# Feed-forward products of two layers as seven quarter products instead of eight (Strassen's scheme), in rounds of 4, 6, 6 and 6 chunks

## The reference, cut to what matters

```python
D_FF = 2816
def swiglu(h, w_gu, w_down):
    gu = h @ w_gu                       # (512 x 1024) @ (1024 x 5632)
    g, u = gu[..., :D_FF], gu[..., D_FF:]
    return (jax.nn.silu(g) * u) @ w_down # (512 x 2816) @ (2816 x 1024)

for i in range(2):
    h = h + (dilated_mixer if i == 0 else forgetting_mixer)(rmsnorm(h, ...), ...)
    h = h + swiglu(rmsnorm(h, ffn_norm[i]), ffn_w_gu[i], ffn_w_down[i])
return rmsnorm(h, final_norm)
```

## Time and profile before

| | |
|---|---|
| median of 3 runs | 2414.19 us (2409.96 to 2414.33) |
| the profiled execution | span 2408.6 us |
| PE busy | 2300.8 us, 96% |
| DVE, ACT, POOL busy | 983.4, 967.8 and 946.0 us, 39 to 41% |
| feed-forward of layer 0 | 1396.2 to 1746.8 us of the span |
| feed-forward of layer 1 | 2052.0 to 2402.6 us of the span |
| DMA | 316 MB, mean 131 GB/s |

### The profile page before, as it was taken

The page is one execution under the profiler, slowest core; times in us unless marked ns, Lnnn a source line. Parts: engine busy times, 40 slices in busy tenths (PEclk is TensorE's granted clock), DMA queues, the critical chain, the costliest instruction groups (busy, mean ns, idle before and its releaser), DMA issues.

```text
span 2408.6 us, 31104 instructions
## 1 busy us (share of the span) xinstructions
PE 2300.8 (96%) x11626; PEld 1871.0 (78%) x11626; DVE 983.4 (41%) x1651; ACT 967.8 (40%) x1611; POOL 946.0 (39%) x757
## 2 busy tenths in 40 slices
PE   7999999888888999999998899999999999999998
PEld 6886786444447998999987688888878887888887
DVE  4377446889884233362235621111311124111113
ACT  4344524656664344344343442222344444322223
POOL 4442141535562333323332145454432222544542
PEclk9999999999999999999998999999999999999999
DMA  5521146999975222322321132333332211333332
GB/s 181 171 87 36 53 163 228 358 390 402 383 310 185 77 88 94 103 69 75 101 89 56 38 103 92 101 96 97 102 106 74 71 53 53 91 102 95 97 100 84
DMA packets 211612, 316.24 MB, mean 131 GB/s; under 512 B 19936, under 2 KB 141536, under 8 KB 201648
## 3 DMA queue, kind: packets, MB, share of 16 engines
q1 hardware_dynamic: 203760, 301.97, 36.5%
q0 software_dynamic: 7744, 12.76, 1.6%
HBM read 300.89 MB, written 22.71 MB: 134 GB/s over the span
## 4 chain that ended last, share of the span: by engine, by line
PE 80%; DVE 6%; DMA 5%; ACT 3%; issue 3%; POOL 1%; SPq 1%; DVEq 0%; ACTq 0%; POOLq 0%
PE bank L868 22%; PE bank L870 21%; PE bank L869 21%; DMA w_ring<-in_w_gate 5%; PE bank L1494 2%; PE bank L1120 2%; PE bank L907 2%; DVE up_low L2555 2%; PE bank L1099 1%; PE bank L1471 1%; POOL w_low L3072 1%; PE bank L1110 1%; PE bank L1481 1%; PE bank L1308 1%; PE bank L1292 1%
## 5 line engine op out<-in xcount | busy, mean ns | idle before, releaser
L3072 POOL TENSOR_TENSOR w_low<-raw,w_high 128x512 fp32r<-128x512 f32 x568 | 743.1, 1339 | 1173.6 <-ACT w_high L1731 1141.8
L868 PE MATMUL bank<-h_high,w_high 128*128 128x512 f32 x1088 | 429.6, 395 | 2.3 <-DVE h_low L2299 2.3
L870 PE MATMUL bank<-h_high,w_low 128*128 128x512 f32 x1088 | 424.4, 390 | 0.0
L869 PE MATMUL bank<-h_low,w_high 128*128 128x512 f32 x1088 | 424.0, 390 | 0.0
L1731 ACT ACTIVATE w_high<-raw 128x2048 fp32r<-128x2048 f32 x145 | 277.0, 1910 | 256.9 <-PE bank L870 237.4
L868 PE MATMUL bank<-w_high,h_high 128*128 128x512 f32 (+2 forms) x832 | 327.9, 394 | 7.7 <-DVE h_low L2299 3.2
L870 PE MATMUL bank<-w_high,h_low 128*128 128x512 f32 (+2 forms) x832 | 312.1, 375 | 0.0
L869 PE MATMUL bank<-w_low,h_high 128*128 128x512 f32 (+2 forms) x832 | 311.8, 375 | 0.0
L868 PEld LDWEIGHTS bank<-h_high,w_high 128*128 128x128 f32 x1088 | 204.6, 188 | 47.2 <-DVE h_low L2299 6.1
L870 PEld LDWEIGHTS bank<-h_high,w_low 128*128 128x128 f32 x1088 | 204.4, 188 | 43.2
L869 PEld LDWEIGHTS bank<-h_low,w_high 128*128 128x128 f32 x1088 | 204.6, 188 | 40.0
(11 more groups left out here) (380 smaller groups left out, 3376.2 us busy)
## 6 DMA issues: line engine op xcount, KB each, us to landing
raw<-in_ffn_w_gu SPq DMA_DIRECT2D x88, 512.0 KB, 4.5
raw<-in_a_w_in SPq DMA_DIRECT2D x72, 512.0 KB, 4.7
w_ring<-in_w_gate SPq DMA_DIRECT2D x35, 1024.0 KB
w_ring<-in_w_up SPq DMA_DIRECT2D x35, 1024.0 KB
w_ring<-in_w_down SPq DMA_DIRECT2D x35, 1024.0 KB, 9.1
raw<-in_ffn_w_down SPq DMA_DIRECT2D x40, 512.0 KB, 4.6
raw<-in_w_in SPq DMA_DIRECT2D x34, 512.0 KB, 4.6
raw<-in_b_w_in SPq DMA_DIRECT2D x24, 512.0 KB, 4.6
```

The source lines that it names most:

```text
L868: pe.matmul(out, sta[0], mov[0], start=start, stop=False)
L869: pe.matmul(out, sta[0], mov[1], start=False, stop=False)
L870: return pe.matmul(out, sta[1], mov[0], start=False, stop=stop)
L3072: last = pool.tensor_tensor(out=w_low[:, slot, cols], in0=raw[:, slot, cols], in1=w_high[:, slot, cols].bitcast(F32), op=ALU.subtract)
```

## The change

A product of two matrices that are cut into 2 x 2 quarters takes eight products of quarters; Strassen's scheme (in Winograd's form) takes seven, of sums of quarters, and combines them with more additions. The new kernel does so for the feed-forward products of 20 of the 22 chunks going up and of all 11 pairs of chunks going down. The first two chunks of a layer (`FF_PLAIN`) go up as before.

**Up.** A chunk's block is a 2 x 2 of (rows 0 to 511, rows 512 to 1023) by (gate, up); h is a 2 x 2 of row halves by token halves. Each of the seven products has 4 k-steps of 128x128 weights on 256 tokens, in three passes. **Down.** A pair of chunks by the two column halves of the down matrix; each product has, for two tiles of 128 tokens, one k-step of 512 columns per pair.

- VectorE makes sums of weight quarters (four 128x512 per chunk; three and a late one per pair), and per layer four sums of quarters of h with their low parts. It combines the seven results in PSUM with 256-wide adds per chunk, and with 22 adds of 128x512 per down round. It makes the sums of the activations per pair of chunks (`act_full`, seven 128x256 and their low part).
- The split parts of weights no longer lie in whole blocks but in a ring of seven quarters of 128x512 (`ring_high`, `ring_low`). ScalarE makes each high part; the low part comes from VectorE for quarters 1 and 2 of an up chunk and 1, 3, 5 of a down pair (`VECTOR_LOW`), otherwise from GpSimd. Each engine's order is one unrolled pass over `FF_QUADS`: at quarter q ScalarE splits q+7, VectorE combines q, makes low parts of q+5 and sums for q+7.
- Rounds are 4, 6, 6, 6 chunks. The down weights of the odd chunks' right and left halves are loaded again for the late quarters, so a layer has 42 blocks for 34.
- Some semaphores are shared by what had its own, the forget gate's weights `fw_raw` and the last gain `gw2` lie elsewhere, tokens are normed in the order 2, 3, 0, 1 after a feed-forward.

```diff
-FF_ROUNDS = [8, 8, 6]
+FF_ROUNDS = [4, 6, 6, 6]
+FF_PLAIN = 2
...
+FF_QUADS = []
+for _r, _chunks in enumerate(FF_ROUNDS):
+    for _c in range(0 if _r else FF_PLAIN, _chunks):
+        FF_QUADS += [("up", _r, _c, _j) for _j in range(7)]
+    for _i in range(_chunks // 2):
+        FF_QUADS += [("down", _r, _i, _j) for _j in range(4)]
+    for _j in range(4, 7):
+        FF_QUADS += [("down", _r, _i, _j) for _i in range(_chunks // 2)]
+VECTOR_LOW = {"up": (1, 2), "down": (1, 3, 5)}
+    ring_high = at("ring_high", 45, [P, 7, 512], F32R)
+    ring_low = at("ring_low", 61, [P, 7, 512], F32R)
...
+            def up_quad(r, c, j):
...
+                quad_ready(q)
...
+                else:
+                    pe.wait_ge(up_read, up0 - 7 + [1, 1, 2, 4, 5, 6, 7][j])
...
+                for k in range(4):
...
+                    last = pass3(out, (wh[:, k, :], wl[:, k, :]), mov, k == 0, k == 3)
+                last.then_inc(quad_used, 1)
...
+            def down_part(r, i, j, tile):
...
+                sta = [x[:, i, ACT_PLACE[j], tile * P:(tile + 1) * P] for x in (act_high, act_low)]
+                return pass3(bank[DOWN_BANKS[j] + tile][:, :], sta, (quad_place(ring_high, q), quad_place(ring_low, q)),
+                             i == 0, i == FF_ROUNDS[r] // 2 - 1)
...
+            def quad_high_part(q):
+                if q >= 7:
+                    act.wait_ge(quad_used, q0 + q - 6)
...
+                act.activation(quad_place(ring_high, q), quad_full(l, q), ACT.Copy).then_inc(quad_high, 1)
...
+            def up_sums(r, c):
...
+                add(s1, a21, a22).then_inc(quad_sum, 1)
+                quad_summed(("up", r, c, 3))
+                sub(s2, s1, a11).then_inc(quad_sum, 1)
+                sub(a21, a11, a21).then_inc(quad_sum, 1)
...
+            def quad_low_part(q):
...
+                dve.wait_ge(quad_high, q0 + q + 1)
+                sub(quad_place(ring_low, q), quad_full(l, q), quad_place(ring_high, q).bitcast(F32))\
+                    .then_inc(vector_low, 1)
...
+            def gated_sums(f):
...
+                step(add(act_full[:, 5, :], act_full[:, 0, :], act_full[:, 4, :]))
+                step(sub(act_full[:, 6, :], act_full[:, 5, :], act_full[:, 1, :]))
+                sub(act_full[:, 7, :], act_full[:, 3, :], act_full[:, 6, :]).then_inc(ff_sums, 1)
...
+            def up_result(r, c, j):
...
+                if j == 1:
+                    add(up_u2[:, :], out, up_first[:, :]).then_inc(up_read, 1)
...
+                elif j == 3:
+                    dve.wait_ge(up_read, up0 + 2)
+                    add(up_c22[:, :], out, up_u3[:, :]).then_inc(up_read, 1)
+                    dve.wait_ge(ff_silu, 2 * f)
+                    add(up_c12[:, :], out, up_u2[:, :]).then_inc(up_read, 1)
...
+            for q in range(FF_N):
+                what, r, i, j = FF_QUADS[q]
+                if what == "up" and j > 0:
+                    up_result(r, i, j)
+                if what == "down":
+                    down_result(r, i, j)
...
+                if q + 7 < FF_N and FF_QUADS[q + 7][3] == 0:
+                    (up_sums if FF_QUADS[q + 7][0] == "up" else down_sums)(*FF_QUADS[q + 7][1:3])
+                if q + 8 < FF_N and FF_QUADS[q + 8][0] == "down" and FF_QUADS[q + 8][3] == 5:
+                    down_last_sum(*FF_QUADS[q + 8][1:3])
+                if q + 5 < FF_N and FF_QUADS[q + 5][3] in VECTOR_LOW[FF_QUADS[q + 5][0]]:
+                    quad_low_part(q + 5)
+                if q + 3 < FF_N and FF_QUADS[q + 3][0] == "up" and FF_QUADS[q + 3][3] == 0:
+                    up_last_sum(*FF_QUADS[q + 3][1:3])
...
+        def quad_lows(l):
+            for q, (what, _, _, j) in enumerate(FF_QUADS):
+                if j not in VECTOR_LOW[what]:
+                    pool.wait_ge(quad_high, FF_N * l + q + 1)
+                    pool.tensor_tensor(out=quad_place(ring_low, q), in0=quad_full(l, q),
+                                       in1=quad_place(ring_high, q).bitcast(F32), op=ALU.subtract).then_inc(pool_low, 1)
```

More of the change, by code:

```diff
@@ L794, in ffn_loads @@
         def ffn_loads(l):
-            w_gu, w_dn = by_k(a["ffn_w_gu_2"][l]), a["ffn_w_down_2"][l]
+            w_gu, w_dn = by_k(a["ffn_w_gu_2"][l]), by_k(a["ffn_w_down_2"][l])
             for r, chunks in enumerate(FF_ROUNDS):
                 n0 = B_FFN[l] + FF_BLOCK[r]
[L799 to L805, removed]
+                pairs = chunks // 2
+                f0 = FF_CHUNK[r]
+                for c in range(chunks):
+                    n = n0 + c
+                    dst = shaped(raw, n % 2, 8)
+                    col = P * (f0 + c)
+                    load(n, n % 2, [(dst[:, :, 0:P], w_gu[:, :, col:col + P]),
+                                    (dst[:, :, P:2 * P], w_gu[:, :, FF + col:FF + col + P])])
                 if l == 0 and r == 0:
@@ L908, in turn, with first_turns @@
             last.then_inc(turned, 1)
-        def first_turns(rows, ready, clock=True):
+        def first_turns(rows, ready, clock=True, order=tuple(range(NT))):
             for m in range(chunk[0], chunk[0] + 2):
@@ L1552, in swiglu @@
         def swiglu(l):
-            for r, chunks in enumerate(FF_ROUNDS):
[L1554 to L1611, removed]
@@ new lines, in swiglu, with first_block @@
+            n0 = B_FFN[l]
+            def first_block(k):
+                if l == 0 and k < 6:
+                    pe.wait_ge(q_low, 3 + k // 2 + 1)
+                elif k == 0 or l == 0:
+                    block_ready(n0)
+                wh, wl = weights(n0 % 2, 8)
+                for m in range(2):
+                    cc = slice(m * P, (m + 1) * P)
+                    last = pass3(PLAIN_BANKS[0][m][:, :], (wh[:, k, cc], wl[:, k, cc]),
+                                 (h_high[:, k, :], h_low[:, k, :]), k == 0, k == KD - 1)
+                if k == KD - 1:
+                    last.then_inc(ff_out, 1)
@@ new lines, in swiglu @@
+            dve.wait_ge(turn_free, chunk[0])
+            for k in range(2):
+                part = slice(4 * k, 4 * k + 4)
+                step(add(h_full[:, part, :], h_high[:, part, :].bitcast(F32), h_low[:, part, :].bitcast(F32)))
+            b11, b12 = h_full[:, 0:4, 0:256], h_full[:, 0:4, 256:512]
+            b21, b22 = h_full[:, 4:8, 0:256], h_full[:, 4:8, 256:512]
+            t1, t2, t3, t4 = [t_full[:, i, :, :] for i in range(4)]
+            sub(t1, b12, b11).then_inc(ff_sums, 1)
```

594 lines of the change are left out of this document (461 added, 133 removed).

## The result

The changed kernel takes 2577.28 us (median of four, 2574.97 to 2578.71) against 2414.26 (2409.96 to 2414.45) for the one before, run beside it: ratio 1.0686, 95% interval 1.067 to 1.0702. The forecast was 2497, its own range 2440 to 2555; the range for 8 in 10, 2370 to 2580, just holds the result. Direction, place and mechanism were as predicted; the loss, 163 us, is twice the 83 forecast.

What follows compares the result with a forecast made beforehand. TensorE's matmul stream bounds the old kernel; in the new one VectorE, stopped by GpSimd's SBUF reads, takes 392 us per layer, 41.4 more than 350.6. Two layers add 83 to 2414.2: 2497 us, range 2440 to 2555, 8 in 10 2370 to 2580.

Steps and rivals of the forecast that it cites:

- The step that failed: Feed-forward stages: VectorE, with GpSimd's stops, paces each layer at 392 us, 41.4 more than 350.6.
- VectorE alone: Feed-forward of a layer: VectorE's own sums, low parts and adds take 291 us, beside TensorE's 320.
- stopped by GpSimd: Feed-forward of a layer: 144 GpSimd instructions each stop VectorE's two-operand SBUF work for 0.70 us.
- VectorE idle: Feed-forward of a layer: VectorE's waits got no term in the 392 us, though full resources were said not to meet without waits.
- w: Feed-forward stages: time one GpSimd instruction stops VectorE, taken as 0.70 us, forecast range 0.50 to 0.90.
- Four prices: VectorE's chunk: stop 0.97 with a two-operand instruction behind, about 0.6 with a lone PSUM add, 0 with three, about 0.65 during PSUM adds.
- The down rounds of three: Down rounds of three pairs: VectorE needs 26.2 us alone, beside 28.6 of TensorE, before GpSimd's stops.
- Rival 2: Feed-forward stages: VectorE and GpSimd alternate strictly, w = 0.97, 431 us per layer, 2575 us; chance 0.11.
- Rival 1: Feed-forward stages: TensorE stays the bound, w at most 0.2, 2358 us; chance 0.18 with its tail up to no change.
- TensorE's 320 us: Feed-forward of a layer: TensorE's matmuls by quarters take 320 us, 30.5 less than before.
- The clock: Granted clock falls with TensorE's idle time; called small, 0.94 to 1.00 at 81 to 88% busy; within a 0.06 rival over 2585 us.
- The forecast's upper case: Each GpSimd instruction stops VectorE for all its 1.26 us: 472 us per layer, 2658 us; a third of a 0.06 chance.

Runs made afterwards that it cites:

- the sums spread: Changed kernel with act_low issued last in its step, plus an up chunk's three weight sums issued in three steps instead of one: 2562.55 us, ratio 1.0637.
- the port free: Changed kernel with GpSimd's quarter low parts replaced by memsets that read no SBUF: 2393.82 us, ratio 0.9928 against the kernel before.
- TensorE alone: Changed kernel with GpSimd's low parts as memsets, and most of VectorE's weight sums cut to 8 of 512 columns: 2387.86 us, ratio 0.9903.
- the better one: Only down products by quarters, all 22 up chunks plain; GpSimd makes a round's first seven low parts, VectorE the others: 2438.35 us, ratio 1.0114.

## Why the prediction was wrong in size

**The step that failed** is the sum "VectorE sets the pace: 291 + 144 x 0.70 = 392 us per layer". It measured 436.5 in layer 0, and the runs split it into its terms:

| term, layer 0 | forecast | measured | from |
|---|---|---|---|
| VectorE alone | 291 | 299.8 | busy time with GpSimd writing only |
| stopped by GpSimd | 101 | 113.0 | busy time of the changed kernel less that |
| VectorE idle | 0 | 23.7 | window less busy time |

That is +9, +12 and +24. (The forecast's prices for dependent instructions hold a gap of 0.04 each, which the last row counts as idle, so the border between the rows isn't sharp.) Both stages together are 436.5 + 432.3 - 2 x 392 = 84.8 us over, and the time 80.

- **Idle time was set at nothing**, and it is the largest piece. A resource that sets the pace was taken to be never idle. The prediction itself wrote that resources full "in any order can't meet without waits", and gave that no price. 9.4 us are waits for ScalarE's high part ahead of act_low, 6.1 for TensorE's results in the down rounds. It is no accident of one order: 20.7 us with act_low last, 24.1 (426.35 - 402.22) with the sums spread, 22.6 with all low parts on VectorE, 29.4 with all on GpSimd. But the waits differ: with all on VectorE 7.6 us of them are late loads, which the changed kernel has none of.
- **w was 0.76 to 0.78, not 0.70** (per 148 or per the 144 counted). In the up chunks alone it is 0.87: ten GpSimd instructions per pair lengthen ten sums and low parts (7.36 us in the chunk shown and 8.14 in the next, in place of 10 x 0.684) by 8.7 us. All 512-wide ones with two SBUF operands last 1.14 in the mean (forecast near 1.0). Four prices under it failed. An instruction directly behind another two-operand one was to lose 0.97, one behind a lone PSUM add 0.6: in the chunk shown they lose 1.09 and 0.76 (1.77 and 1.44 in place of 0.68). Longer runs of PSUM adds were to cover the stop whole; spreading the sums showed that it falls on the next two-operand instruction instead. And all adds of down results were priced as PSUM adds, while 32 of a layer's are X<-down_u with two SBUF operands: 32 x (918 - 683) = 7.5 us.
- **VectorE alone** was 3% short. That the 0.09 by which independent instructions overlap isn't reached in every place is a guess; no run shows it. From the measured 299.8, 144 more instructions at the forecast's 0.60 came out within 2% (386 for 380.0).
- **What held:** VectorE busy over 85% (95%); TensorE waiting for VectorE's low parts, not for GpSimd, ScalarE or loads; 256-wide PSUM adds at 0.42; 256-column matmuls 0.12 apart; GpSimd's 128x512 over 1.5 (1.63). The down rounds of three, 35.1 for 34.6, are in part luck, since the slowed X<-down_u weren't in their price.
- **Rival 2** named 2575 us, 2 from the result, for another reason: strict alternation at w = 0.97. The slowest sums do last 1.77 in the trace, but the mean is 0.76 and the rest is idle time.
- **Rival 1** (2358) had more against it than the port: with the port free 2393.8, and with TensorE alone 2387.9. That TensorE's 320 us would be met but for late starts was too low by 17 a layer.
- **The clock** was called small. It was granted at 0.91 and 0.90 in the two stages, where TensorE mostly didn't set the pace. In one place it did: at the end of round 0 TensorE had waited 7.11 us for act_low, its next matmuls ran 0.43 apart at a granted clock of 0.50 (1453.5 to 1459.0; that is the 1.2 GHz level) in place of 0.23, and VectorE waited 4.86 us for their result, the longest of its waits:

```profile
1454.13 0.79 PE L978 MATMUL bank<-ring_high,act_high 128*128 128x512 f32 x1 [7.11 <-DVE act_low L2486]
```
```profile
1459.54 1.29 DVE L2483 TENSOR_TENSOR X<-down_u,X 128x512 f32<-128x512 f32 x2 [4.86 <-PE bank L980]
```

What stays open: of the remaining 8.2 us of VectorE's idle time in layer 0, 1.5 are a wait for ScalarE's root at the end, the rest some 110 gaps of 0.11 us or less, whose cause isn't shown. Open, too, is whether the down half alone could win with the squares ahead of the split and GpSimd's plain blocks held back. By an estimate from the waits shown that would give back about 4 us each a layer, not enough for the 27 that the better one lacks. It wasn't tried.

## What to carry to other kernels

Trading matmuls for elementwise work moves the bound to VectorE; price that work with GpSimd's SBUF reads beside it, and count for each instruction how many operands lie in SBUF, the copies that were made to free PSUM too. A low part given to GpSimd cost VectorE 0.7 to 0.8 us here, more than the 0.56 of making it itself. When several engines come out 80 to 100% full in one loop, add idle time to the fullest (5 to 7% here) before comparing with a margin of that size.

## What the runs showed of the hardware

- The stop between VectorE and GpSimd goes both ways. VectorE's 1792-wide act_low lasts 2.02 us in the changed kernel and with GpSimd only writing; where a GpSimd instruction starts 0.57 behind it, it is GpSimd's that lasts 2.59 in place of about 1.3, as in these two lines of the kernel with the sums spread:

```profile
1508.16 2.02 DVE L2486 TENSOR_TENSOR act_low<-act_full,act_high 128x1792 fp32r<-128x1792 f32 x1 [1.08 <-ACT act_high L2361]
```
```profile
1508.73 2.59 POOL L3611 TENSOR_TENSOR ring_low<-t_place,ring_high 128x512 fp32r<-128x512 f32 x1 [6.11 <-ACT ring_high L2335]
```

- The longest stop of a single 512-wide sum in the chunk shown is 1.77 - 0.68 = 1.09 us, of a GpSimd instruction of about 1.3 unhindered, so a single stop comes near the whole instruction. The mean per GpSimd instruction is 0.76: behind a PSUM add the stop is 0.76 rather than 1.09, and 0.25 where VectorE comes late (0.93). The forecast's upper case took the whole 1.26 for each of them, which wasn't reached.
- After a wait of 3.84 us TensorE's matmuls ran 3.7 us at the 1.2 GHz level (granted clock 0.54), after the one of 7.11 us they did so for 5 us (0.50). Each of these two waits cost more than its length.
